# Attention in a two-layer hybrid decoder: the order of scores and transposes on TensorE, and of minimum and copies on VectorE

## The chip, the core and the metric

The kernel runs on one core of one Trainium2 chip. The core has TensorE (matrix products and transposes into PSUM), VectorE, ScalarE, GpSimd and SyncE (which here issues DMAs). Each engine runs its own instructions in program order and waits on semaphores where it needs the work of another. The metric is the device time of one execution in microseconds; lower is better.

## What is computed

A decoder trunk of two layers over 1024 positions of width 1024. Each layer projects its input, sends the columns to three groups (an SSD scan, causal latent attention with 4 heads, sliding-window attention with 4 heads, window 128 and a learned sink for each head), projects their outputs back and then runs a gated MLP. The part that the change touches are the two attentions:

```python
# latent attention, swept over 128-query blocks i, heads h of 4
sc = jnp.einsum('bqhd,bkhd->bhqk', qi, k) * scale          # keys up to block i
sc = jnp.where(kpos[None, :] <= qpos[:, None], sc, -jnp.inf)
pr = jax.nn.softmax(sc, axis=-1)
o  = jnp.einsum('bhqk,bkhd->bqhd', pr, v)

# banded attention: block i sees the key blocks i-1 and i, and a sink
sc = jnp.where(valid, sc, -jnp.inf)
pr = jax.nn.softmax(jnp.concatenate([sc, sink], axis=-1), axis=-1)[..., :-1]
o  = jnp.einsum('bnhgqk,bnkhd->bnqhgd', pr, vb)
```

## The kernel before

In each layer the attention is cut into 32 units (NU), numbered 0 to 31 and written u below. A latent unit ("m") holds one query block and two heads while the block has at most 512 keys, later one head with up to 1024 keys. A banded unit ("s") holds one query block and all four heads. The eight banded units are u = 4, 7, 9, 12, 15, 22, 25 and 28. Everything is float32, and a unit passes through these steps:

- `scores(u)`, TensorE (L1310 for s, L1320 for m): products into PSUM `bank[u % 2]`. It first waits for `un_e` of unit u-2 (L1304), which had that bank. The queries are scaled by a negative number, so a minimum takes the place of the softmax's maximum.
- `least(u)`, VectorE: for m, the mask is taken off the diagonal block in the bank (L2323), then the minimum of each row (L2324). For s, one subtraction carries all four heads from the bank into the SBUF tile `swaProb` (L2316), then the minimum (L2318).
- `exps(u)`, ScalarE: for m, one exponential for each head from the bank into `prob` (L1859), which also waits for the transposes of u-2. For s, four exponentials inside `swaProb` (L1854). The last one signals `un_e`.
- `transposes(u)`, TensorE (L1352 for m, L1347 for s): 128x128 blocks of the probabilities into `bank[2]`. It waits for `un_e` of u and, since there is one bank for all units, for both copies of unit u-1.
- `copy_probs(u)`: the turned blocks go from `bank[2]` to SBUF (L734), one part by ScalarE (`un_ca`), the other by VectorE (`un_cd`).
- `values(u)`, TensorE (L1380 for m, L1371 for s): probabilities times values. An m unit whose head is the first of a pair that is split over two units has none of its own: the second unit does both. Behind the last unit of a query block, `inverse_sums` (L1387) spreads the inverses of the row sums.

ScalarE's order in its loop over u is written out by hand and has a special case: where unit u+1 is latent it runs `exps(u+1)` and then its copy of u; where unit u+1 is banded it runs the copy of u first and then `exps(u+1)`. `finish()` behind them holds small work (the copy of the spread inverses L1872, `att_hi` L1877, and at some units a root or a rounding of SSD outputs). VectorE's loop ends with small work too: the reciprocal of the sums (L2329), the scaling of the outputs (`att_scaled`, L2340) and `att_lo` (L2346), a subtraction of two SBUF tiles.

TensorE's loop before, for each u: transposes(u), scores(u+2), values(u-1), inverse_sums(u-1). VectorE's loop before: copy of u, least(u+2), then the small work. GpSimd meanwhile does other things (adaLN products for the next layer, the SSD outputs' normalisation) that no step here waits for.

The order on ScalarE, which the change leaves as it is:

```python
if u + 1 < NU and UNITS[u + 1][0] == "s":
    copy_probs(act, u, "a", "un_ca")
    exps(u + 1)
    finish()
    continue
if u + 1 < NU:
    exps(u + 1)
if u < NU:
    copy_probs(act, u, "a", "un_ca")
finish()
```

Of the kernel before, what the change touches and what calls it, by code (L numbers as in the profile page):

```python
# [169 lines left out]
NU = len(UNITS)  # L170
# [47 lines left out]
def build(nc, x, c, positions, ada_w, ada_b, norm1_g, norm2_g, w_in, ssd_conv_w, ssd_conv_b,  # L218
# [142 lines left out]
    def half(pair, i):  # L361
        return bank[pair][:, HALF * i:HALF * (i + 1)]
# [17 lines left out]
    def nth(name, v):  # L380

        return passed.get(name, 0) + v
# [293 lines left out]
    def trunk_layer(block, layer):  # L676
# [377 lines left out]
        def _(pe):  # L1054
# [244 lines left out]
            def scores(u):  # L1299
                kind, i, hs = UNITS[u]  # L1300
                if u < 2:
                    pe.wait_ge(s["mp_kv"], nth("mp_kv", 6 + 2 * u))
                else:
                    pe.wait_ge(s["un_e"], nth("un_e", u - 1))  # L1304
                if kind == "s":
                    lo = max(i - 1, 0) * BLK
                    for h in range(SWA_H):
                        r = slice(64 * (h // 2), 64 * (h // 2) + 64)
                        o = bank[u % 2][:, h * 256 + (0 if i else BLK):(h + 1) * 256]
                        last = mm(o, sq[r, h % 2, i * BLK:(i + 1) * BLK], sk[r, lo:(i + 1) * BLK], start=True, stop=True)  # L1310
                else:
                    if u == 0:
                        pe.wait_ge(s["rope_dve"], nth("rope_dve", 3))
                        pe.wait_ge(s["k_rope"], nth("k_rope", 16 * 3))
                        pe.wait_ge(s["mp_q"], nth("mp_q", 12))
                    n = (i + 1) * BLK
                    for q, h in enumerate(hs):
                        for a in range(0, n, HALF):
                            b = min(a + HALF, n)
                            last = mm(bank[u % 2][:, q * HALF + a:q * HALF + b], qh[h][0:96, i * BLK:n], kh[h][0:96, a:b], start=True, stop=True)  # L1320
                last.then_inc(s["un_s"], 1)
# [7 lines left out]
            def transposes(u):  # L1329
                kind, i, hs = UNITS[u]  # L1330
                pe.wait_ge(s["un_e"], nth("un_e", u + 1))
                if u >= 1:
                    pe.wait_ge(s["un_ca"], nth("un_ca", u))
                    pe.wait_ge(s["un_cd"], nth("un_cd", u))
                else:
                    pe.wait_ge(s["mp_kv"], nth("mp_kv", 10))
                if u in SUMS_AT:
                    square_sums(SUMS_AT.index(u))
                if u == TURN_AT:
                    pe.wait_ge(s["sd_rstd"], nth("sd_rstd", 3))  # L1340
                    pe.transpose(half(2, 1)[0:2 * NB, 384:512], rst[:], ident[:])
                if u in NEXT_AT and onward:
                    ada_sum(4 + NEXT_AT.index(u))
                if kind == "s":
                    for h in range(SWA_H):
                        for b in range(0 if i else 1, 2):
                            last = pe.transpose(bank[2][:, (2 * h + b) * P:(2 * h + b + 1) * P], prs[i % 2][:, h, b * P:(b + 1) * P], ident[:])  # L1347
                else:
                    for q in range(len(hs)):
                        for b in range(i + 1):  # L1350
                            c0 = slice(q * HALF + b * P, q * HALF + (b + 1) * P)
                            last = pe.transpose(bank[2][:, c0], pr[u % 2][:, c0], ident[:])  # L1352
                last.then_inc(s["un_t"], 1)
# [29 lines left out]
            def inverse_sums(kind, i):  # L1383

                pe.wait_ge(s["sw_r" if kind == "s" else "ml_r"], nth("sw_r" if kind == "s" else "ml_r", i + 1))
                for h in range(4):
                    last = mm(att_bank(kind)[64 * (h % 2):64 * (h % 2) + 64, 256 + (h // 2) * P:256 + (h // 2 + 1) * P],  # L1387
                              stat[kind][:, i % 3, 2, h:h + 1].to_broadcast([P, 64]), ident[:], start=True, stop=True)
                last.then_inc(s["sw_b" if kind == "s" else "ml_b"], 1)
# [10 lines left out]
            def out_steps(t, ks):  # L1400

                if ks[0] == 0:
                    pe.wait_ge(s["split_lo"], nth("split_lo", splits(N_OUT0 + t)))
                for k in ks:
                    if t == 0:
                        sem, v = ("sd_lo", k + 1) if k < 4 else ("ml_lo" if k < 6 else "sw_lo", NB)
                        pe.wait_ge(s[sem], nth(sem, v))
                    last = dense_step(t, k, tile_of(N_OUT0 + t, wHi), tile_of(N_OUT0 + t, wLo), y_hi_of, y_lo_of, k == 0, k == 5)
                if ks[-1] == 5:
                    last.then_inc(s["pack_used"], 1)  # L1410

            scores(0)
            scores(1)
            for u in range(NU + 1):
                if u < NU:
                    transposes(u)
                if u + 2 < NU:
                    scores(u + 2)
                if u == NU:
                    out_steps(0, (1, 2))  # L1420
                if u >= 1:
                    values(u - 1)
                    kind, i, _ = UNITS[u - 1]
                    if LAST[kind][i] == u - 1:
                        inverse_sums(kind, i)
                if u == NU - 2:
                    out_steps(0, (0,))
# [646 lines left out]
        def _(dve):  # L2074
            step = [0]

            def link(ins):

                step[0] += 1
                ins.then_inc(s["dve_step"], 1)  # L2080
                dve.wait_ge(s["dve_step"], nth("dve_step", step[0]))
# [224 lines left out]
            def least(u):  # L2306
                kind, i, hs = UNITS[u]
                dve.wait_ge(s["un_s"], nth("un_s", u + 1))
                st_ = stat[kind][:, i % 3]
                if kind == "s":  # L2310
                    dve.wait_ge(s["sw_m"], nth("sw_m", 2 + i))
                    if i >= 2:
                        dve.wait_ge(s["un_t"], nth("un_t", LAST["s"][i - 2] + 1))
                    lo = 0 if i else BLK
                    s4 = bank[u % 2][:].rearrange("p (h k) -> p h k", h=4)[:, :, lo:256]
                    link(dve.tensor_tensor(prs[i % 2][:, :, lo:256], s4, band[:].rearrange("p b k -> p (b k)")[:, lo:256].unsqueeze(1).to_broadcast([P, 4, 256 - lo]),  # L2316
                                           ALU.subtract))
                    dve.tensor_reduce(st_[:, 0, :], prs[i % 2][:, :, lo:257], AX.X, ALU.min).then_inc(s["un_n"], 1)  # L2318
                else:
                    n, k = (i + 1) * BLK, len(hs)  # L2320
                    sc = bank[u % 2][:].rearrange("p (q n) -> p q n", q=k)
                    diag = sc[:, :, i * BLK:n]
                    link(dve.tensor_tensor(diag, diag, band[:, 1, :].unsqueeze(1).to_broadcast([P, k, P]), ALU.subtract))  # L2323
                    dve.tensor_reduce(st_[:, 0, hs[0]:hs[0] + k], sc[:, :, 0:n], AX.X, ALU.min).then_inc(s["un_n"], 1)  # L2324
# [24 lines left out]
            def beside_probs(u):  # L2349

                sums = half(2, 1)
                dve.wait_ge(s["un_t"], nth("un_t", u + 1))
                if u == SUMS_AT[1]:
                    dve.tensor_copy(rst[:], sums[:, 384:384 + 2 * NB]).then_inc(s["sd_rstd"], 1)
                if u == TURN_AT:
                    dve.tensor_copy(rstd_row[:], sums[0:2 * NB, 384:512]).then_inc(s["sd_rstd"], 1)
                if u in NEXT_AT and onward:
                    n = NEXT_AT.index(u)
                    dve.tensor_copy(mod[:, n * KT:(n + 1) * KT], sums[:, 384:384 + KT]).then_inc(s["mod_rest"], 1)
# [3 lines left out]
            for u in range(NU + 3):  # L2363
                if u in (SUMS_AT[1], TURN_AT) + NEXT_AT:
                    beside_probs(u)
                if u < NU:
                    copy_probs(dve, u, "d", "un_cd")
                if u == INV_AT:
                    inverse(rst[:], "sd_rstd", 2)
                if u + 2 < NU:  # L2370
                    least(u + 2)
                for w, todo in ((u, inverse_of), (u - 1, att_scaled), (u - 3, att_lo)):
                    if 0 <= w < NU and LAST[UNITS[w][0]][UNITS[w][1]] == w:
                        todo(UNITS[w][0], UNITS[w][1])
# [318 lines left out]
```

## Time and profile before

| | |
|---|---|
| time, 3 runs | 2361.38, 2367.51, 2369.55 us (median 2367.51) |
| the profiled execution's own time | 2360.93 us |
| its span, first to last instruction | 2359.2 us (1.7 us lie around it) |
| mean granted TensorE clock | 0.991 of 2.4 GHz |
| busy share of the span | TensorE 97%, weight loads 79%, VectorE 69%, ScalarE 47%, GpSimd 43% |
| attention of layer 0 | about 350 to 458 us |
| attention of layer 1 | about 1499 to 1604 us |

A row of the timeline is a run of equal instructions: its start, how long from the first start to the last end, engine, line, what it writes and reads, how many. In square brackets stands how long the engine had been idle and who released it. Ends of TensorE's rows are modelled, and a row can overlap the next one by some 0.17 us, since matmuls are pipelined; the distance between two starts is the safer length.

### The profile page before, as it was taken

Reading aid. Unit: us, or ns where it says so; the run is one execution under the profiler, and the core shown is the slowest. Engines: PE = TensorE matmul, PEld = TensorE weight load, DVE = VectorE, ACT = ScalarE, POOL = GpSimd, SP = SyncE. Lnnn points to the kernel's source line nnn. Section 1 sums busy time; section 2 is a strip of 40 time slices with the busy share of each in tenths; the row PEclk is TensorE's granted clock in tenths of the full one; section 3 lists DMA queues with packets and bytes.
Section 4 is the critical chain, followed back from the end, with each engine's and each line's share of the span. In section 5 each row is a group of like instructions: output and inputs, shape, how many; then the busy total and the mean of one; then the engine's idle time right before and its main releaser. Section 6 shows DMA issues by size and latency. Waiting matters only on the chain.

```text
span 2359.2 us, 31193 instructions
## 1 busy us (share of the span) xinstructions
PE 2283.9 (97%) x11493; PEld 1853.1 (79%) x11493; DVE 1633.9 (69%) x2084; ACT 1100.3 (47%) x1808; POOL 1013.5 (43%) x641
## 2 busy tenths in 40 slices
PE   5999999999899999999999999999989999999998
PEld 5788866788788888888878888568878888888887
DVE  6974467638876766777898544773697667677886
ACT  4334646524444444444552454573444444445455
POOL 1211268534887777400002123242479777760000
PEclk7999999999999999999999999999999999999999
DMA  8651213242333333487546331004413333347763
GB/s 292 224 187 54 77 52 126 99 139 85 92 112 90 112 89 118 145 292 254 154 176 206 108 85 54 7 20 152 143 41 125 112 90 112 90 130 254 245 214 112
DMA packets 272533, 310.71 MB, mean 132 GB/s; under 512 B 36872, under 2 KB 191230, under 8 KB 271358
## 3 DMA queue, kind: packets, MB, share of 16 engines
q1 hardware_dynamic: 272094, 307.94, 40.4%
q8 instruction: 92, 1.51, 0.3%
q10 hardware_dynamic: 288, 0.79, 0.2%
q14 instruction: 59, 0.48, 0.1%
HBM read 246.47 MB, written 61.42 MB: 131 GB/s over the span
## 4 chain that ended last, share of the span: by engine, by line
PE 80%; DVE 10%; ACT 3%; issue 2%; POOL 1%; DMA 1%; DVEq 0%; SPq 0%; ACTq 0%; POOLq 0%
PE bank L1489 30%; PE bank L1504 17%; PE bank L1062 15%; PE bank L1122 5%; PE bank L1320 2%; DVE nt L2178 2%; PE bank L1352 1%; PE bank L1280 1%; DVE hLo L2132 1%; PE bank L1380 1%; DVE hLo L2118 1%; DVE xT L2126 1%; DMA raw<-in_ffn_w_up_dram 1%; PE bank L1209 1%; PE bank L1131 1%
## 5 line engine op out<-in xcount | busy, mean ns | idle before, releaser
L982 POOL TENSOR_TENSOR wLo<-raw,wHi 128x1024 fp32r<-128x1024 f32 x66 | 161.9, 2454 | 456.0 <-ACT wHi L984 456.0
L1679 POOL TENSOR_TENSOR prodLo<-comb,prodHi 128x512 fp32r<-128x512 f32 x160 | 234.3, 1471 | 123.6 <-ACT prodHi L1024 123.6
L1489 PE MATMUL bank<-tHi,prodHi 128*128 128x512 f32 x640 | 249.7, 390 | 6.1 <-DVE tLo L2487 4.1
L1489 PE MATMUL bank<-tLo,prodHi 128*128 128x512 f32 x640 | 249.0, 389 | 0.0
L1489 PE MATMUL bank<-tHi,prodLo 128*128 128x512 f32 x640 | 249.0, 389 | 0.0
L1504 PE MATMUL bank<-gateHi,downHi 128*128 128x512 f32 x616 | 240.3, 390 | 0.0
L1504 PE MATMUL bank<-gateHi,downLo 128*128 128x512 f32 x616 | 239.7, 389 | 0.0
L1504 PE MATMUL bank<-gateLo,downHi 128*128 128x512 f32 x616 | 239.7, 389 | 0.0
L1024 ACT ACTIVATE prodHi<-comb 128x512 fp32r<-128x512 f32 x160 | 100.5, 632 | 248.8 <-PE bank L1489 228.7
L2432 DVE SCALAR_TENSOR_TENSOR ub<-bank,ffp,ub 128x1023 f32<-128x1023 f32 x88 | 112.8, 1282 | 141.8 <-ACT ub L1940 140.2
L1489 PE MATMUL bank<-hHi,prodHi 128*128 128x512 f32 x480 | 187.1, 390 | 6.9 <-POOL prodLo L1679 4.3
L1062 PE MATMUL bank<-hHi,wHi 128*128 128x512 f32 x576 | 187.5, 407 | 3.0 <-POOL wLo L982 2.1
L1489 PE MATMUL bank<-hLo,prodHi 128*128 128x512 f32 x480 | 186.8, 389 | 0.0
L1489 PE MATMUL bank<-hHi,prodLo 128*128 128x512 f32 x480 | 186.8, 389 | 0.0
L984 ACT ACTIVATE wHi<-raw 128x1024 fp32r<-128x1024 f32 x66 | 69.5, 1056 | 245.1 <-PE bank L1062 170.2
L1062 PE MATMUL bank<-hLo,wHi 128*128 128x512 f32 x576 | 178.5, 391 | 0.0
L1062 PE MATMUL bank<-hHi,wLo 128*128 128x512 f32 x576 | 177.5, 389 | 0.0
L1679 POOL TENSOR_TENSOR prodLo<-raw,prodHi 128x512 fp32r<-128x512 f32 x120 | 165.3, 1404 | 0.0
L1489 PEld LDWEIGHTS bank<-tHi,prodHi 128*128 128x128 f32 x640 | 120.1, 188 | 33.0 <-DVE tLo L2487 5.0
L1489 PEld LDWEIGHTS bank<-tHi,prodLo 128*128 128x128 f32 x640 | 120.1, 188 | 25.1
L1489 PEld LDWEIGHTS bank<-tLo,prodHi 128*128 128x128 f32 x640 | 120.1, 188 | 24.7
L1504 PEld LDWEIGHTS bank<-gateHi,downHi 128*128 128x128 f32 x616 | 115.7, 188 | 24.4 <-issue 0.8
(392 smaller groups left out, 5402.1 us busy)
## 6 DMA issues: line engine op xcount, KB each, us to landing
raw<-in_ffn_w_up_dram SPq DMA_DIRECT2D x88, 512.0 KB, 5.1
gateRaw<-gateOut SPq DMA_DIRECT2D x154, 256.0 KB, 4.1
adaE<-in_ada_w_dram SPq DMA_DIRECT2D x64, 512.0 KB, 5.7
gateOut<-gateSums SPq DMA_DIRECT2D x22, 1024.0 KB, 5.4
raw<-in_w_in_dram SPq DMA_DIRECT2D x34, 512.0 KB, 4.4
downRaw<-in_ffn_w_down_dram SPq DMA_DIRECT2D x66, 256.0 KB, 3.6
raw<-in_w_out_dram SPq DMA_DIRECT2D x28, 512.0 KB, 4.1
downCols<-in_ffn_w_down_dram SPq DMA_DIRECT2D x24, 512.0 KB, 3.8
```

The costliest lines, as they stand in the source:

```text
L982: eng.tensor_tensor(lo[:], raw[slot][:], fview(hi[:]), ALU.subtract).then_inc(s["split_lo"], 1)
L984: eng.activation((early_hi if n in (N_OUT0, N_PRE + 2) else third_hi if n == 2 else wHi[slot])[:], raw[slot][:], ACT.Copy).then_inc(s["spl ...
L1024: act.activation(sHiW[idx][:], product_source(js, idx), ACT.Copy).then_inc(s["us_hi"], 1)
L1062: last = mm(half(pair, hf), w(k), r(k)[:, HALF * hf:HALF * (hf + 1)], start=first and q == 0, stop=last_k and q == 2)
L1122: last = mm(o, w[n % 2][:, k * P:(k + 1) * P], r(k)[:, cols], start=first and q == 0, stop=last_k and q == 2)
L1131: last = mm(to[:, m:m + 1], acc[:, m * P:(m + 1) * P], caus01[:, P - 1:P], start=True, stop=True)
L1320: last = mm(bank[u % 2][:, q * HALF + a:q * HALF + b], qh[h][0:96, i * BLK:n], kh[h][0:96, a:b], start=True, stop=True)
L1489: last = mm(o, w[idx][:, c0], moving(idx, kp, hi), start=kp == 0 and q_ == 0, stop=kp == 3 and q_ == 2)
L1504: last = mm(down_bank(p, m), w[ring(n)][:, m * P:(m + 1) * P], g[ring(n)][:], start=i == 0 and q == 0, stop=i == NK - 1 and q == 2)
L1679: pool.tensor_tensor(sLoW[idx][:], product_source(js, idx), fview(sHiW[idx][:]), ALU.subtract).then_inc(s["us_lo"], 1)
L2178: ins = dve.scalar_tensor_tensor(out=acc[:], in0=adaE[j][k][:], scalar=cact[:, k:k + 1], in1=acc[:], op0=ALU.mult, op1=ALU.add)
L2432: dve.scalar_tensor_tensor(out=y[:, d:T], in0=bank[2 * q + b][:, 0:T - d], scalar=ffp[:, col:col + 1], in1=y[:, d:T], op0=ALU.mult, op1=AL ...
```

## The change

TensorE issues the scores of unit u+2 ahead of the transposes of unit u, and VectorE runs the minimum of unit u+2 ahead of its copy of unit u. Waits, buffers, the amount of work and the order on ScalarE, GpSimd and SyncE stay.

```diff
@@ TensorE
             scores(0)
             scores(1)
             for u in range(NU + 1):
+                if u + 2 < NU:
+                    scores(u + 2)
                 if u < NU:
                     transposes(u)
-                if u + 2 < NU:
-                    scores(u + 2)
                 if u == NU:
                     out_steps(0, (1, 2))
                 if u >= 1:
@@ VectorE
             for u in range(NU + 3):
                 if u in (SUMS_AT[1], TURN_AT) + NEXT_AT:
                     beside_probs(u)
+                if u + 2 < NU:
+                    least(u + 2)
                 if u < NU:
                     copy_probs(dve, u, "d", "un_cd")
                 if u == INV_AT:
                     inverse(rst[:], "sd_rstd", 2)
-                if u + 2 < NU:
-                    least(u + 2)
                 for w, todo in ((u, inverse_of), (u - 1, att_scaled), (u - 3, att_lo)):
```

## Rows read from the trace of the kernel before

**Rows 1.** The page's part 4: engines' shares of the chain that ended last.

```profile
PE 80%; DVE 10%; ACT 3%; issue 2%; POOL 1%; DMA 1%; DVEq 0%; SPq 0%; ACTq 0%; POOLq 0%
```

**Rows 2.** Windows (length, busy PE, PEld, DVE, ACT, POOL, clock, DMA): both attentions, a pause.

```profile
350.00:458.00 108.00, 102.13 (x901) 74.64 (x901) 81.14 (x144) 74.48 (x206) 85.63 (x40) 1.00 0.30 91
1499.00:1604.00 105.00, 98.81 (x869) 70.80 (x869) 79.68 (x142) 74.49 (x206) 28.86 (x13) 1.00 0.06 20
348.00:353.00 5.00, 3.30 (x19) 2.93 (x20) 1.80 (x5) 2.92 (x12) 4.92 (x3) 1.00 0.35 108
```

**Rows 3.** Waits, 345 to 450 us (waiter, whom for: total us, times, longest).

```profile
PE bank L1352 <- ACT probT L734: 2.5, 3, 1.1
PE bank L1352 <- ACT prob L1859: 2.0, 2, 1.4
PE bank L1347 <- ACT swaProb L1854: 0.8, 1, 0.8
```

**Rows 4.** Timeline, TensorE, around banded unit 12 (transposes 11 to transposes 12).

```profile
388.73 0.74 PE L1352 MATMUL bank<-ident,prob 128*128 128x128 f32 x5 [0.58 <-ACT prob L1859]
389.30 1.25 PE L1320 MATMUL bank<-mlaK,mlaQ 96*128 96x512 f32 x4
390.48 1.09 PE L1380 MATMUL bank<-probT,mlaV 128*64 128x128 f32 x16
391.40 0.61 PE L1387 MATMUL bank<-ident,stat_m 128*64 128x128 f32 x8
392.12 1.09 PE L1347 MATMUL bank<-ident,swaProb 128*128 128x128 f32 x8
```

**Rows 5.** Timeline, ScalarE, same place: copy of 11, first exponential, last accumulator of 12.

```profile
389.50 0.60 ACT L734 ACTIVATE probT<-bank 128x512 f32<-128x512 f32 x1 [0.60 <-PE bank L1352]
389.99 0.50 ACT L1854 ACTIVATE swaProb<-swaProb,stat_s 128x257 f32<-128x257 f32 x1
...
391.87 0.19 ACT L1854 ACTIVATION_READ_ACCUMULATOR swaProb<-swaProb,stat_s 128x1 f32 x1
```

**Rows 6.** Timeline, TensorE, around banded unit 7: transposes 6, values 5, transposes 7.

```profile
370.45 0.85 PE L1352 MATMUL bank<-ident,prob 128*128 128x128 f32 x6
...
372.95 0.88 PE L1380 MATMUL bank<-probT,mlaV 128*64 128x128 f32 x12
373.85 1.09 PE L1347 MATMUL bank<-ident,swaProb 128*128 128x128 f32 x8
```

**Rows 7.** Timeline, TensorE, around banded unit 4: transposes 3, values 2, transposes 4.

```profile
358.39 0.66 PE L1352 MATMUL bank<-ident,prob 128*128 128x128 f32 x4
...
360.27 0.66 PE L1380 MATMUL bank<-probT,mlaV 128*64 128x128 f32 x8
361.06 0.66 PE L1347 MATMUL bank<-ident,swaProb 128*128 128x128 f32 x4
```

**Rows 8.** Timeline, TensorE, around banded unit 15: transposes 14, values 13, transposes 15.

```profile
397.78 0.76 PE L1352 MATMUL bank<-ident,prob 128*128 128x128 f32 x5
...
399.56 1.31 PE L1380 MATMUL bank<-probT,mlaV 128*64 128x128 f32 x20
401.70 1.09 PE L1347 MATMUL bank<-ident,swaProb 128*128 128x128 f32 x8 [0.83 <-ACT swaProb L1854]
```

**Rows 9.** Timeline, TensorE: transposes 21, values 20, and values 26.

```profile
420.43 0.95 PE L1352 MATMUL bank<-ident,prob 128*128 128x128 f32 x7 [1.14 <-ACT probT L734]
...
422.82 1.53 PE L1380 MATMUL bank<-probT,mlaV 128*64 128x128 f32 x24
...
447.30 1.75 PE L1380 MATMUL bank<-probT,mlaV 128*64 128x128 f32 x28
```

**Rows 10.** Timeline, ScalarE: last accumulator of banded unit 22.

```profile
423.79 0.19 ACT L1854 ACTIVATION_READ_ACCUMULATOR swaProb<-swaProb,stat_s 128x1 f32 x1
```

**Rows 11.** Timeline, VectorE, before transposes 20 and 21: att_lo, then the copy of 19.

```profile
414.51 2.38 DVE L2346 TENSOR_TENSOR swaLo<-attOut,swaHi 128x256 fp32r<-128x256 f32 x1
...
416.81 0.41 DVE L734 COPY probT<-bank 128x256 f32<-128x256 f32 x1
```

**Rows 12.** Groups by line, VectorE, 350 to 458 us (busy us, mean ns | idle before).

```profile
L2318 DVE TENSOR_REDUCE stat_s<-swaProb 128x4 f32<-128x1028 f32 (+1 forms) x8 | 9.3, 1157 | 0.3
L2316 DVE TENSOR_TENSOR swaProb<-bank,band 128x1024 f32<-128x1024 f32 (+1 forms) x8 | 9.2, 1152 | 1.9 <-PE bank L1310 1.8
...
L2346 DVE TENSOR_TENSOR swaLo<-attOut,swaHi 128x256 fp32r<-128x256 f32 x7 | 6.2, 890 | 0.0
L2346 DVE TENSOR_TENSOR mlaLo<-attOut,mlaHi 128x256 fp32r<-128x256 f32 x7 | 5.0, 714 | 0.0
```

## The prediction

> **What bounds the kernel now.** First the chain of work that ended last: TensorE holds 80% of it [rows 1]. So a microsecond that TensorE idles inside the attention is a microsecond of the whole, and the question is only what the new order does to TensorE's idle time. Second the windows of the two attentions: TensorE is busy 102.13 of 108 us in layer 0 and 98.81 of 105 in layer 1 [rows 2]. It idles 5.87 and 6.19 us, 12.1 together. That is all a new order can win, 0.5% of the time. Third the waits: what is late is always ScalarE, with its copies (2.5 us), its latent exponentials (2.0) and its banded ones (0.8) [rows 3]. VectorE is late only through it. Last the timeline around a banded unit, where the case is decided.
>
> **What moves.** No instruction is added or taken away. On TensorE scores(u+2) goes ahead of transposes(u), one pass of 1.2 to 1.8 us ahead of one of 0.5 to 1.0. Both wait for the exponentials of u, and the transposes alone also for the copies of u-1. Behind each exponential the chain scores, minimum, exponentials of u+2 starts one transposition earlier, which looks like a gain. But read as a ring the order is now: transposes(u), values(u-1), inverse sums, scores(u+3), transposes(u+1). The exponentials of u+1 were wanted by transposes(u+1), behind all of these; now they are wanted by scores(u+3), one pass of scores sooner.
>
> For a latent unit that costs nothing in steady state: ScalarE runs its exponentials before the copy of u, so they need only the minimum and the transposes of u-1, and are done early. For a banded unit ScalarE's program has the copy of u in front, and this copy needs transposes(u). The chain transposes(u), copy, four exponentials is now wanted at scores(u+3), and between lie only values(u-1) and perhaps the inverse sums.
>
> **The price of one banded unit.** Unit 12 shows the chain bare [rows 4, 5]. Transposes 11 start at 388.73 and last 0.74. The copy starts at 389.50, the first exponential 0.49 later at 389.99, and the last accumulator read ends at 391.87 + 0.19 = 392.06. Transposes 12 start at 392.12, so the chain is 3.39 us, or 2.65 behind the modelled end of the transposes. Unit 22 agrees: 420.43 to 423.79 + 0.19 = 423.98 is 3.55, plus 0.06 is 3.61, minus 0.95 is 2.66 [rows 9, 10]. In rows 4 TensorE filled these 3.39 us with transposes (0.57 between starts), scores 13 (1.18), values (0.92) and inverse sums (0.6), so before it just fits. Take the scores away from between and 1.3 us stay open.
>
> In general the next thing on TensorE can start 0.17 us before a modelled end (0.74 against 0.57, 1.09 against 0.92, both [rows 4]). So the hole is 2.65 + 0.17 = 2.82 us, less the values' busy time less 0.17, less 0.54 where inverse sums stand there (0.61 less 0.07). By unit:
>
> - unit 4: chain 361.06 - 358.39 = 2.67, less 0.66 is 2.01, plus 0.17, less values 0.49: 1.69 [rows 7]
> - unit 7: chain 3.40, less 0.85 is 2.55, plus 0.17, less values 0.71: 2.01 [rows 6]
> - units 9 and 12: 2.82 - 0.92 - 0.54 = 1.36 each [rows 4]
> - unit 15: 2.82 - 1.14 = 1.68 (no inverse sums) [rows 8]
> - unit 22: 2.82 - 1.36 - 0.54 = 0.92 [rows 9]
> - unit 25: 2.82 - 1.58 = 1.24; unit 28: 2.82 - 1.58 - 0.54 = 0.70 [rows 9]
>
> The sum is 10.96 us a layer. The minimum of a banded unit (1.15 + 1.16 us [rows 12]) is asked for before its exponentials by the length of a whole unit, and doesn't lengthen these chains.
>
> **What stays of the old idle time.** The longest wait, 1.4 us for the very first exponentials [rows 3], has nothing that could be put before it and stays. The 0.58 us at unit 11 [rows 4] is a busy ScalarE in front of unit 11's exponentials; it is now met by scores 13: about 0.5. The 0.83 at unit 15 [rows 8] is inside the 1.68 above. The 1.14 at unit 21 [rows 9] begins with an att_lo of 2.38 us [rows 11], and may go or come back.
>
> **What VectorE's half costs.** Its copy of u now stands behind the minimum of u+2. Transposes(u+1) wait for that copy. Between transposes(u) and transposes(u+1) TensorE has values(u-1) and scores(u+3). The worst regular place is u = 20: unit 22 is banded, its minimum takes 2.3 us and unit 19 has no values. From the end of scores 22 VectorE needs 2.3 + 0.1 + 0.4 (copy as in rows 11) = 2.8, and TensorE has transposes 20 and scores 23, some 0.7 + 1.6: 0.5 to 0.6 open. Among the first units, where passes are short, copy 0 behind minimum 2 holds back transposes 1: I lay the first five units out and find 0.7 us of idle where 1.1 was. Bounds for all of VectorE's half: from 0 (all hidden, as most are) to 5.5 us a layer, which is what its att_lo take beyond 0.41 each (11.2 us for 14 [rows 12]), if each such delay now met a waiting TensorE. I take 1.6 (0.6, 0.7 and 0.3 for a late att_lo), nearer zero, because in all of rows 3 no TensorE wait is put down to VectorE.
>
> **Sum.** New idle a layer: 10.96 + 1.4 + 0.5 + 1.6 = 14.5 us. Old: 5.87 and 6.19. Difference 8.6 + 8.3 = 16.9 us. On the profiled execution, 2360.93 us with 1.7 around the span, that is 2377.8. This execution lies at the lower end of the three runs (2361.38 to 2369.55), so against their median the forecast is 2367.5 + 16.9 = 2384.4, given as 2384. Little can absorb it: behind the attention the output projection starts on TensorE without a gap, and its weights are there before.
>
> **Rivals.**
> *The order does what it is shaped for* and the banded hole isn't there, because the copy and exponentials fit beside the values. The old waits but the first go: 12.1 - 2 x 1.4 = 9.3 us, so 2358. For it speaks that the loop scores, minimum, exponentials does get one transposition shorter. Against it stands rows 4 and 5: 3.39 us are measured between transposes 11 and 12, and only 2.1 us of TensorE's work is left in them. It decides if ScalarE's chain were shorter than about 2.1 us.
> *Even:* the stall is there but something later had to wait anyway, so that no more than 7 us arrive at the end: 2367 to 2374. The output projection would have to wait for a weight or for the SSD part, which GpSimd and DMA bring at their own time. Against it: 80% of the chain is TensorE.
> *VectorE becomes the bound:* its att_lo is seen at 2.38 us [rows 11] against some 0.4, and whatever is queued behind it is late. With the minimum now also in front of the copy, both reach transposes(u+1). If all that lock-like time counts, 5.5 us a layer instead of 0.3, the result is 2384 + 10 = 2394. The Trainium skill (page "SBUF — State Buffer", section "Who interferes with whom") has a rule for this that speaks against the change: a VectorE instruction with two SBUF inputs and a GpSimd instruction that reads SBUF exclude each other for a whole instruction. By that rule att_lo (two SBUF inputs) waits and the copies and minima, which have one, don't; the trace agrees, since copies stay at 0.41.
>
> **Chances.** Forecast 0.78, even 0.10, faster 0.06, VectorE as bound 0.06. The forecast's own range: with 1 us less of holes a layer and VectorE's half at zero, 16.9 - 2 - 3.2 = 11.7, from the lowest run 2373; with 2 us more a layer and the highest run, 2369.55 + 20.9 = 2390. For the third rival I reach to 2393. A measurement here can tell about 0.3% (7 us) from no change: faster 0.06, same 0.10, slower 0.84.
>
> **What would show it.** In the changed kernel's waits, scores (L1310 and L1320, two lines on or off) must wait for ScalarE's banded exponentials, eight times a layer and some 11 us in a layer, with 2 us at unit 7 and under 1 at unit 28. The windows of the attentions must be 8 us longer at equal busy time of TensorE. Latent exponentials should release little but at the start. Wrong would be: scores that find the bank free behind banded units; a window that grows while TensorE waits mostly for VectorE's copies; or a granted clock under 1.00 there, which I exclude because it stays at 1.00 where TensorE is busy only 3.30 of 5 us [rows 2].

## The result and the profile after

The changed kernel takes 2382.59 us (median of 4 runs, 2381.83 to 2383.73) where the kernel before took 2367.47 (4 runs, 2361.38 to 2369.55). The recorded ratio is 1.0080, 95% interval 1.0067 to 1.0092, so slower beyond doubt. These two medians alone are only 15.1 us or 0.64% apart, because the four runs of the kernel before scatter by 8 us and three of them lie high: in the runs beside the experiments below (15, 23 and 27 of them) its median is 2364.28, 2364.36 and 2363.70 us, and from those the changed kernel is 18.2 to 18.9 us away. The forecast was 2384, in a range of 2373 to 2393. The execution whose profile is shown took 2382.1 us, 21.2 over the profiled one of before; why that is more than 15.1 is told below.

The page of the changed kernel has the same number of instructions on TensorE, VectorE, ScalarE and GpSimd as before and the same order in the chain that ended last. Its first lines (part 1: busy time, share of the span, instructions) and the chain, which answers to [rows 1]:

```profile
span 2380.3 us, 31195 instructions
PE 2295.1 (96%) x11493; PEld 1863.7 (78%) x11493; DVE 1629.5 (68%) x2084; ACT 1101.0 (46%) x1808; POOL 1013.9 (43%) x641
PE 80%; DVE 10%; ACT 3%; issue 3%; POOL 1%; DMA 1%; DVEq 0%; SPq 0%; ACTq 0%; POOLq 0%
```

The place of the loss is in the windows. I take each attention from the start of its first scores to the start of the output projection behind it. Windows of the changed kernel (length, then busy PE, PEld, DVE, ACT, POOL, granted clock, DMA), layer 0 and layer 1:

```profile
350.40:471.77 121.37, 108.16 (x919) 79.72 (x917) 80.22 (x144) 75.42 (x207) 85.28 (x40) 0.97 0.27 85
1511.46:1625.85 114.39, 101.35 (x886) 73.33 (x885) 77.26 (x142) 75.36 (x207) 29.02 (x13) 1.00 0.06 22
```

The same two stretches of the kernel before:

```profile
350.13:459.16 109.03, 103.16 (x919) 75.53 (x917) 81.27 (x144) 75.11 (x207) 85.50 (x40) 1.00 0.31 95
1498.75:1605.00 106.25, 100.06 (x887) 71.87 (x885) 79.68 (x142) 75.00 (x207) 28.86 (x13) 1.00 0.07 23
```

Layer 0 is 12.34 us longer, layer 1 is 8.14 us longer: 20.5 of the 21.1 us between the two spans. The rest of the program is 0.6 us longer. TensorE's waits in layer 1 of the changed kernel (waiter, whom for: total us, times, longest), to be read against [rows 3]:

```profile
PE bank L1320 <- ACT swaProb L1854: 7.5, 7, 1.4
PE bank L1352 <- DVE probT L734: 2.1, 5, 0.7
PE bank L1310 <- ACT swaProb L1854: 1.7, 1, 1.7
PE bank L1320 <- ACT prob L1859: 1.6, 2, 1.4
```

Before, no scores waited for anything; it was transposes that waited, for ScalarE's copies and exponentials. Now eight scores a layer, lines L1310 and L1320, wait for the exponentials of a banded unit, 9.2 us together. Layer 0 has the same two rows, 7.5 and 1.7. The place of [rows 4] and [rows 5] in the changed kernel, unit 12, TensorE first:

```profile
395.78 0.74 PE L1352 MATMUL bank<-ident,prob 128*128 128x128 f32 x5
396.45 1.09 PE L1380 MATMUL bank<-probT,mlaV 128*64 128x128 f32 x16
397.38 0.61 PE L1387 MATMUL bank<-ident,stat_m 128*64 128x128 f32 x8
399.17 1.35 PE L1320 MATMUL bank<-mlaK,mlaQ 96*128 96x512 f32 x4 [1.19 <-ACT swaProb L1854]
```

and ScalarE and VectorE in the same stretch:

```profile
396.56 0.60 ACT L734 ACTIVATE probT<-bank 128x512 f32<-128x512 f32 x1 [1.48 <-PE bank L1352]
397.05 0.50 ACT L1854 ACTIVATE swaProb<-swaProb,stat_s 128x257 f32<-128x257 f32 x1
...
398.10 0.28 DVE L734 COPY probT<-bank 128x128 f32<-128x128 f32 x1
...
398.93 0.19 ACT L1854 ACTIVATION_READ_ACCUMULATOR swaProb<-swaProb,stat_s 128x1 f32 x1
```

Read it from above: transposes 11 start at 395.78, ScalarE's copy starts as soon as they are done (396.56; ScalarE had idled 1.48 us for them), four exponentials follow without a gap, the read of the last accumulator ends at 399.12, and 0.05 us later scores 14 start. From the transposes' start that is 399.17 - 395.78 = 3.39 us, to the hundredth what [rows 4] showed between transposes 11 and 12. TensorE has values and inverse sums in it, and no longer scores.

The other difference is the clock. In layer 0 TensorE's granted clock falls twice to 0.5, the 1.2 GHz level, which the profiled execution of before doesn't do there. Windows of the changed kernel around the two falls, and most of the stretch between them:

```profile
378.00:382.00 4.00, 4.00 (x31) 3.40 (x30) 3.13 (x4) 1.34 (x5) 2.63 (x2) 0.57 0.46 146
382.00:437.00 55.00, 48.70 (x420) 34.67 (x421) 39.50 (x70) 36.99 (x96) 38.84 (x19) 1.00 0.27 87
439.00:444.00 5.00, 5.00 (x34) 3.83 (x33) 4.05 (x6) 1.93 (x3) 4.37 (x3) 0.66 0.00 0
```

Against full speed the first loses 4 x 0.43 = 1.7 us, the second 5 x 0.34 = 1.7 us. By this estimate 3.4 of layer 0's 12.34 us are clock, and 8.9 are left beside layer 1's 8.14.

### The profile page after: what moved, and what is told of

It reads as the page before. It is cut to its first block, busy times and chain, and to the rows that moved or that the text cites. A ratio compares the mean times of both kernels' runs of the same rounds, so it can differ in the third digit from the quotient of the medians.

```text
span 2380.3 us, 31195 instructions
## 1 busy us (share of the span) xinstructions
PE 2295.1 (96%) x11493; PEld 1863.7 (78%) x11493; DVE 1629.5 (68%) x2084; ACT 1101.0 (46%) x1808; POOL 1013.9 (43%) x641
## 4 chain that ended last, share of the span: by engine, by line
PE 80%; DVE 10%; ACT 3%; issue 3%; POOL 1%; DMA 1%; DVEq 0%; SPq 0%; ACTq 0%; POOLq 0%
PE bank L1489 30%; PE bank L1504 17%; PE bank L1062 15%; PE bank L1122 5%; PE bank L1320 3%; DVE nt L2178 2%; PE bank L1352 1%; ACT swaProb L1854 1%; PE bank L1280 1%; DVE hLo L2132 1%; PE bank L1380 1%; DVE hLo L2118 1%; DVE xT L2126 1%; DMA raw<-in_ffn_w_up_dram 1%; PE bank L1209 1%
```

## The experiments

Theory A is the prediction's: in the new order scores(u+3) want the exponentials of a banded unit u+1, which ScalarE runs only behind its copy of u, and the chain transposes, copy, exponentials (3.39 us) no longer fits under what TensorE has to do. The rivals are named in the expectations. Every ratio is to the kernel before, run on the same chip beside it, with its 95% interval.

### TensorE's half alone

```diff
 (VectorE as before)
+                if u + 2 < NU:
+                    scores(u + 2)
                 if u < NU:
                     transposes(u)
-                if u + 2 < NU:
-                    scores(u + 2)
```

> TensorE's half alone: scores of u+2 ahead of the transposes of u, VectorE in its old order. Theory A (the banded holes: TensorE's scores wait for ScalarE's copy and four banded exponentials, one after the other): the eight holes a layer stay as in the changed kernel, 0.5 to 1.8 us each and 9.2 us together, and only the waits for VectorE's copies (about 2 us a layer) go: 2377 to 2381. Theory B (VectorE's half costs the time, by its late copies): about 2367, as before.

Measured: 2375.97 us, ratio 1.0049 (1.0036 to 1.0061). TensorE's waits in layer 1:

```profile
PE bank L1320 <- ACT swaProb L1854: 7.9, 7, 1.4
PE bank L1310 <- ACT swaProb L1854: 1.7, 1, 1.7
PE bank L1320 <- ACT prob L1859: 1.6, 2, 1.4
PE bank L1310 <- ACT prob L1859: 1.0, 1, 1.0
```

The eight holes are there with VectorE in its old order, so they are TensorE's half: theory B falls as the main cause. The waits for VectorE's copies (2.1 us in the changed kernel) are gone, and one of 1.0 us for a latent unit's exponentials has come. The time is 1 us under the expected band. The rest of the way to 1.0080 belongs to VectorE's half. With falls of the clock taken off (1.7 us in this run's layer 1, 3.4 in the changed kernel's layer 0) its two attentions are 116.6 and 112.6 us long against 117.95 and 114.39: 3.1 us. The 6.6 us between the medians aren't explained by that alone. A second part is probably the clock: the changed kernel's runs have mean clocks of 0.989 to 0.990 and four of these five 0.991 or 0.992. No run here holds the clock fixed, so how the 6.6 us divide stays open.

### VectorE's half alone

```diff
 (TensorE as before)
+                if u + 2 < NU:
+                    least(u + 2)
                 if u < NU:
                     copy_probs(dve, u, "d", "un_cd")
...
-                if u + 2 < NU:
-                    least(u + 2)
```

> VectorE's half alone: minimum of u+2 ahead of the copy of u, TensorE in its old order. The copy now waits for the scores, which stand behind the transposes, and then for a minimum of 1.3 us (latent) or 2.4 (banded); TensorE has only values and inverse sums to cover it. Worked out over the units that is some 0.5 us for most, near 1.9 for each where values are missing (8 a layer) and 1.7 in front of each banded one: 30 us a layer, 2410 to 2440. Theory A expects this, since it holds the two halves for one move that has to be made together. Theory B expects about the changed kernel's 2383.

Measured: 2473.23 us, ratio 1.0458 (1.0444 to 1.0473). The expected direction and cause, but nearly twice the size. TensorE's waits in layer 0, and the window of that attention:

```profile
PE bank L1352 <- DVE probT L734: 24.6, 16, 3.0
PE bank L1347 <- DVE probT L734: 4.3, 5, 1.5
PE bank L1131 <- DVE probT L734: 3.7, 2, 2.3
PE bank L1327 <- DVE probT L734: 3.4, 2, 2.3
PE bank L1341 <- DVE probT L734: 2.0, 1, 2.0
```

```profile
349.76:512.00 162.24, 122.30 (x918) 86.22 (x916) 81.72 (x144) 76.37 (x207) 84.87 (x40) 0.88 0.21 66
```

The waits for VectorE's copies are 38 us in the layer where 30 were worked out. What I had left out is the last column but two: with pauses of up to 3 us the granted clock averages 0.88, and the same products (918 in this window, 919 in that of before) are busy 122.3 us where they were 103.2. Of the 53.2 us by which this attention is longer than before, 34.1 are idle time and 19.1 busy time. The two halves are one move: VectorE's half without TensorE's is far worse than either kernel.

### Old order at the banded unit's own iteration

```diff
+                banded = u < NU and UNITS[u][0] == "s"
-                if u + 2 < NU:
+                if u + 2 < NU and not banded:
                     scores(u + 2)
                 if u < NU:
                     transposes(u)
+                if u + 2 < NU and banded:
+                    scores(u + 2)
 (and the same for VectorE's minimum and copy)
```

> The changed kernel, but at the eight iterations of a layer whose own unit is banded both engines keep the old order (transposes, scores; copy, minimum). Theory A: the scores that had the holes are again behind the transposes, so the holes go and the time is 2360 to 2369. Theory B: 24 of 32 iterations still have VectorE's copy behind the minimum, so most of the loss stays: 2376 to 2382.

Measured: 2380.32 us, ratio 1.0060 (1.0047 to 1.0074). Theory A's expectation failed, by an error of mine, and the time lies where theory B had it. The waits speak against theory B all the same. TensorE's waits in layer 1:

```profile
PE bank L1347 <- ACT swaProb L1857: 9.2, 8, 1.7
PE bank L1352 <- DVE probT L734: 2.3, 4, 0.8
PE bank L1320 <- ACT prob L1862: 1.4, 1, 1.4
```

The holes are all there with their old sizes (9.2 us, eight of them) but stand in front of the banded transposes (L1347). That is what theory A really says: the hole is set by what lies between transposes(u) and the first instruction that needs the exponentials of u+1. Scores(u+2) had already gone ahead of transposes(u), in the iteration before, and it doesn't matter which instruction then meets the wait.

### ScalarE runs banded exponentials first

```diff
-                if u + 1 < NU and UNITS[u + 1][0] == "s":
-                    copy_probs(act, u, "a", "un_ca")
-                    exps(u + 1)
-                    finish()
-                    continue
                 if u + 1 < NU:
                     exps(u + 1)
                 if u < NU:
                     copy_probs(act, u, "a", "un_ca")
```

> The changed kernel with ScalarE's special case taken out: it runs the exponentials of a banded u+1 ahead of its copy of u, as it does for latent units. Theory A: all eight holes a layer go (18.4 us), copies of ScalarE are up to 2 us later at banded units but the scores now lie in front of the transposes that need them; what stays is the first 1.4 us and small waits: 2358 to 2368. Theory C (scores that come early must wait for some exponentials whatever ScalarE's order is, and lost time is the clock's): 2378 or more.

Measured: 2361.76 us (11 runs), ratio 0.9989 (0.9980 to 0.9998), inside the expected band. Its waits in layer 1:

```profile
PE bank L1352 <- DVE probT L734: 2.1, 5, 0.7
PE bank L1320 <- ACT prob L1859: 1.6, 2, 1.4
PE bank L1347 <- DVE probT L734: 0.5, 1, 0.5
```

No wait for a banded exponential is left; the two rows that held 9.2 us are gone, the first two rows are those of the changed kernel, and one wait of 0.5 us for a copy of VectorE has come. Nothing of the change was undone, so its whole loss hangs on ScalarE's order of its copy and its banded exponentials. Theory C falls, its part on the clock too: in this profile the clock falls twice in layer 0, as in the changed kernel's, and the time is still that of before. The same edit on the kernel before is the control:

> The kernel before with nothing but ScalarE's special case taken out. Theory A: before, the chain copy and banded exponentials just fitted under scores, values and inverse sums, so its order is worth little: the 0.8 us at unit 15 and some tenths elsewhere go, but ScalarE's copy is late for the next transposes in places: 2361 to 2368, within 0.15% of before. Theory E (ScalarE's order is worth the same with or without the change): 2350 or less.

Measured: 2369.35 us, ratio 1.0016 (1.0007 to 1.0024): there it costs some 4 us, a little more than expected. The wait for banded exponentials that was to go has grown, from 0.8 us [rows 3] to 1.8 in layer 0. So each order on TensorE has its own best order on ScalarE, and the kernel before had its own.

### The bank given back at the minimum

```diff
-                    pe.wait_ge(s["un_e"], nth("un_e", u - 1))
+                    free = "un_n" if UNITS[u - 2][0] == "s" else "un_e"
+                    pe.wait_ge(s[free], nth(free, u - 1))
```

> The changed kernel with another wait for the scores that follow a banded unit in its bank: they wait for its minimum, which is behind the last read of the bank, and not for its exponentials. ScalarE's order stays. Theory A: the scores go at once and fill the hole; the transposes of the banded unit wait for the exponentials behind scores, values and inverse sums, as before the change. Holes under 0.3 us: 2358 to 2367. Theory C (ScalarE's order itself costs the time, by late copies): 2375 or more.

Measured: 2372.97 us, ratio 1.0034 (1.0021 to 1.0048), only half way: over theory A's 2358 to 2367 and under the 2375 of theory C, which here says that ScalarE's order costs time by late copies. Waits in layer 1 (its lines stand one lower):

```profile
PE bank L1321 <- ACT prob L1860: 3.1, 4, 1.4
PE bank L1353 <- DVE probT L734: 2.1, 5, 0.7
...
PE bank L1311 <- ACT prob L1860: 1.3, 2, 0.7
PE bank L1348 <- ACT swaProb L1855: 0.7, 1, 0.7
```

The scores no longer wait for banded exponentials. But the latent exponentials behind them on ScalarE are late in turn, and the next scores wait for those (1.4 us of the 4.4 are the first unit's, as ever). A part of the hole was handed on, so theory A left something out. Theory C's late copies of ScalarE don't show: no row names them; what is late are exponentials. With ScalarE's order mended as well, the freed bank should add nothing:

> Both mends at once: ScalarE runs banded exponentials ahead of its copy, and the scores behind a banded unit wait only for its minimum. Theory A: with ScalarE's order mended the bank is free in time anyway, so the second mend adds nothing: ratio to before as with the first alone, 0.998 to 0.9998. If waiting for the bank still cost something: under 0.997.

Measured: 2364.08 us, ratio 0.9998 (0.9989 to 1.0007), at the upper edge of the expected band. It isn't better than ScalarE's order alone.

### A longer chain

```diff
                 if u + 1 < NU and UNITS[u + 1][0] == "s":
                     copy_probs(act, u, "a", "un_ca")
+                    if u == 3:
+                        act.wait_ge(s["sd_y"], nth("sd_y", NB))
+                    A(spare[:, UNITS[u + 1][1], :]..., ident[:]..., ACT.Copy)      # 128x256
                     exps(u + 1)
```

> The changed kernel with one more ScalarE copy (128x256, to a tile nobody reads) between its copy of u and the exponentials of a banded u+1. It is worth 0.3 to 0.4 us of ScalarE. Theory A: the chain has no slack, so each of the eight holes a layer grows by just that (1.19 to about 1.55 at unit 12) and the kernel gets 5 to 6.5 us slower than the changed one: a ratio to before of 1.009 to 1.011. If the holes had another cause, ScalarE is busy 46% and would hide it: ratio 1.006 to 1.008 as for the changed kernel.

Measured: 2389.25 us, ratio 1.0108 (1.0094 to 1.0122). Its ScalarE and TensorE at unit 12 (lines a few lower):

```profile
397.10 0.60 ACT L735 ACTIVATE probT<-bank 128x512 f32<-128x512 f32 x1 [1.22 <-PE bank L1353]
...
397.59 0.41 ACT L1900 ACTIVATE spareOut<-ident 128x256 f32<-128x256 f32 x1
397.90 0.50 ACT L1855 ACTIVATE swaProb<-swaProb,stat_s 128x257 f32<-128x257 f32 x1
...
400.02 1.35 PE L1321 MATMUL bank<-mlaK,mlaQ 96*128 96x512 f32 x4 [1.50 <-ACT swaProb L1855]
```

The added copy takes 0.31 us from start to start, and the hole is 1.50 us where it was 1.19. So it is at all eight units: 1.42 became 1.73, 1.74 became 2.04, 1.41 became 1.71, 0.75 became 1.06, 0.97 became 1.28, 0.53 became 0.84. Sixteen times 0.31 is 5.0 us; the medians lie 6.7 apart. The chain has no slack at all, on an engine that is busy 46% of the span.

### Old order one iteration ahead

```diff
+                banded_next = u + 1 < NU and UNITS[u + 1][0] == "s"
-                if u + 2 < NU:
+                if u + 2 < NU and not banded_next:
                     scores(u + 2)
                 if u < NU:
                     transposes(u)
+                if u + 2 < NU and banded_next:
+                    scores(u + 2)
```

With both engines turned back so:

> The changed kernel, but with the old order on both engines in the eight iterations of a layer before a banded unit (u + 1 banded), the other iterations new. Keeping the old order at the banded unit's own iteration moved the eight holes from the scores to the transposes and left their sizes. Theory A, made sharper by that: a hole is 2.8 us less TensorE's work between transposes(u) and whatever first needs the exponentials of u+1. Here scores(u+2) stand between again, 1.2 to 1.8 us, so the holes go or stay under 0.3 us: 2359 to 2367. Theory B (VectorE's half, still new in 24 of 32 iterations): 2374 or more.

Measured: 2383.20 us, ratio 1.0079 (1.0065 to 1.0094). That is far over theory A's 2359 to 2367 and in theory B's band (2374 or more). The holes for banded exponentials are gone but one of 0.33 us, and in layer 1 TensorE now waits like this:

```profile
PE bank L1352 <- DVE probT L734: 9.0, 9, 2.2
PE bank L1320 <- ACT prob L1862: 1.4, 1, 1.4
PE bank L1352 <- ACT probT L734: 0.8, 1, 0.8
```

Where a new iteration is followed by an old one, transposes(u-1) and transposes(u) have no scores between them, and VectorE's copy, which stands behind a minimum, is late: 9.0 us, the size of what was mended. Here theory B is right: this loss is VectorE's half. Another part of the time is clock: in layer 0 of this profile it is at the lower level for 10.2 us in all, an estimated 5.1 us lost. With VectorE's order the old one throughout:

> TensorE's half alone, with TensorE's old order in the eight iterations of a layer before a banded unit; VectorE's order is the old one throughout. The run that did this with both halves lost its gain to VectorE's copies (up to 2.2 us each), because where a new iteration is followed by an old one no scores stand between two transpositions. With VectorE's copy in front of its minimum that can't happen. Theory A: the 18 us of holes of TensorE's half alone (0.49% over before) go, 2358 to 2366, no wait of scores for banded exponentials over 0.3 us. Theory F (a hole just moves to the next unit, whatever is done on TensorE): 2373 or more.

Measured: 2366.52 us, ratio 1.0008 (0.9999 to 1.0017). Of the 0.49% of TensorE's half alone 0.08 are left, so theory F falls; but the median is 0.5 us over the band, and two waits of 0.25 and 0.77 us for banded exponentials stayed in layer 0, where none over 0.3 was expected. Waits of 1.5 to 1.8 us for ScalarE's and VectorE's copies appear at such seams.

### Two candidates

TensorE's half with ScalarE's order mended and VectorE's left alone:

> TensorE's half alone with ScalarE's special case taken out (banded exponentials ahead of the copy), VectorE in its old order. Theory A: no holes from ScalarE, and none of the 2 us a layer that TensorE waits for VectorE's copies when both halves are new: 2 to 4 us under the run with both halves and this ScalarE order, 2356 to 2361. Theory D (with ScalarE's order mended VectorE's half is worth having, since least is then what is late): 2363 or more.

Measured: 2364.58 us, ratio 1.0005 (0.9997 to 1.0014), in theory D's band. The waits agree with it: in layer 1 the scores again wait 2.6 us for banded exponentials, and none did with both halves. And both halves with VectorE's old order only at the first unit and where the unit two on is banded:

```diff
+                late = u == 0 or (u + 2 < NU and UNITS[u + 2][0] == "s")
-                if u + 2 < NU:
+                if u + 2 < NU and not late:
                     least(u + 2)
                 if u < NU:
                     copy_probs(dve, u, "d", "un_cd")
...
+                if u + 2 < NU and late:
+                    least(u + 2)
```

> A candidate: both halves new, ScalarE's special case taken out, and VectorE's old order (copy, then minimum) only at the first unit and at the eight iterations where the unit two on is banded, whose minimum takes 2.4 us. Theory A: of the waits for VectorE's copies that are left with both halves (0.45, 0.3, 0.5, 0.7, 0.4 and 0.3 us, some 2.8 a layer) most go: 2 to 5 us under the run with both halves and this ScalarE order, ratio to before 0.997 to 0.9985. Theory D (these minima are then late for ScalarE): ratio 0.999 or more.

Measured: 2365.73 us, ratio 1.0008 (0.9999 to 1.0017). I was wrong here too: the ratio lies in theory D's band (0.999 or more). Some waits for VectorE's copies are gone, but in layer 0 it waits for exponentials again:

```profile
PE bank L1320 <- ACT prob L1859: 1.8, 2, 1.4
PE bank L1320 <- ACT swaProb L1854: 1.6, 3, 0.8
PE bank L1310 <- ACT prob L1859: 1.4, 2, 1.0
```

With ScalarE's order mended the early minimum is worth having, and the best kernel of all is the changed one with ScalarE's special case removed, 0.11% (0.02 to 0.20) under the kernel before. That gain is barely clear of noise.

## Why the prediction was right

**What bounds the kernel.** Right. The two attentions carry 20.5 of the 21.1 us between the spans, and no later stage took anything back.

**The price of a banded unit.** The mechanism is shown by the holes' place, by the edit of ScalarE's order that removes them, and by the longer chain that enlarges each by its own length. The sizes were 1.69, 2.01, 1.36, 1.36, 1.68, 0.92, 1.24 and 0.70 us; the profile shows 1.42, 1.74, 1.19, 1.19, 1.41, 0.75, 0.97 and 0.53, that is 9.2 a layer in place of 10.96. The chain itself was exact (3.39 us). What was off is the cover, always by the same: 0.27 us where only values stand in it, 0.17 where inverse sums do too. At unit 12 transposes that are followed by values occupy TensorE 0.67 us (395.78 to 396.45), where I had 0.57 from [rows 4], in which scores follow them; and the profile counts a pause from the modelled end, 0.17 us (values) or 0.07 (inverse sums) after the next instruction could have started. The second part is no gain, only another way to count.

**What stays.** The 1.4 us at the first unit stayed (1.38). The 0.5 at unit 11 was 0.23. The wait at unit 15 went into its hole as said.

**VectorE's half.** Taken at 1.6 us a layer; the waits for its copies are 2.1 in layer 1 and 2.3 in layer 0, and with TensorE's half alone the two attentions are 3.1 us shorter, 1.6 a layer. The two places worked out came true: 0.71 us in front of transposes 21 (forecast 0.5 to 0.6), 0.46 at transposes 1 (0.7 in all at the first units). The choice near the lower bound was right, since the upper bound had been 5.5. One reason given for it was too broad: [rows 3] cover layer 0 alone, and in layer 1 of the kernel before TensorE waits 0.9 us for VectorE's copies (two waits, 0.5 and 0.4).

**The sum.** For layer 1, where the clock is full in both profiles, 8.3 us were forecast and 8.14 measured. That is partly luck: the shown waits are 12.9 us where 14.5 were forecast, and busy time grew by 1.3 us (100.06 to 101.35) where I had assumed equal. By line, the latent scores (L1320) are busy 36.6 us in place of 34.8, and all transposes 27.0 in place of 27.8. For layer 0 8.6 were forecast and 8.9 measured with the clock's 3.4 taken off. That 2384 came within 1.5 us of the median measured is luck in part as well. The forecast added its 16.9 us to a median of three runs of before that was 3.2 to 3.8 us higher than the later ones, and holes forecast 1.8 us a layer too large stood against busy time and a clock that it had put at nothing.

**What was wrong.** The last sentence of the forecast excludes a clock under 1.00 in the attention, from one stretch where it had stayed full. It fell twice in layer 0 of this execution. The difference of the profiled executions is 21.2 us; without the clock's 3.4 it is 17.8, 0.9 over the 16.9 of the sum. The medians on record with the result are 15.1 apart, and 18.2 to 18.9 with the later medians of before.

**The rivals.** The gain that the order is shaped for does exist but is small: with the holes mended the whole move is worth 0.11%, where the rival had 0.4%. "Even" fell with the windows. VectorE did not become the bound while TensorE's half was made with it; alone it did, at 1.0458.

## What to carry to other kernels

When an instruction is put ahead of another in a software pipeline, list for every engine that is not touched which of its instructions now lies on the shortened way; here it was a special case for eight units of 32 in ScalarE's order, right for the old order and wrong for the new. The hole can be worked out before a run: the chain's length between two starts, less what the waiting engine still has to do in it, and it doesn't matter which instruction meets the wait. A mend is a change of the other engine's order, not of the place where the wait shows: two attempts to turn the order back locally on both engines only moved the hole, to the transposes or to VectorE's copies, and a third, on TensorE alone, did no more than bring back the time of before. Freeing the bank earlier, where the wait shows, won half.

## What the runs showed of the hardware

The granted clock falls to the 1.2 GHz level within both attentions, in nearly every order of the work that was tried, mostly for some 3.5 us at a time, and such a fall costs an estimated 1.7 us. The longest outside VectorE's half alone lasts 10 us (from 1521 us, ScalarE's order changed in the kernel before). Twelve of the fourteen profiles have stretches in layer 0 or 1 that windows of a microsecond show at 0.50 (366 to 369 and 431 to 434 us with ScalarE's order mended, 1534 to 1537 with TensorE's half alone); the profile of before and that of the second run under "Old order one iteration ahead" have none.

In all profiles but that of VectorE's half alone, each fall begins beside or within 5 us behind one of the groups of 16 products of a single column (L1327 and L1131), of which each profile has four in layer 0 and two in layer 1. With ScalarE's order mended such groups start at 364.18 and 428.52 us and last some 1.9, and the first low windows are those of 366 and 431; in the changed kernel they start at 371.78 and 437.02, and the falls begin at about 378, behind a pause of 1.74 us as well, and at about 439.7. But the 78 groups of these 13 profiles have only 21 falls behind them, and the profile of before has all six groups and no fall. So these groups may have a part in it, and pauses too; no run here takes them apart, and the cause stays open.

It isn't tied to the change. Of the 65 executions of the kernel before beside the experiments, the fastest (2360.58 us) has a mean clock of 0.992 and the slowest (2371.22 us) one of 0.987, and over all of them time and clock go against each other (correlation -0.83), so most of the scatter between its executions goes with the clock.

With pauses of up to 3 us the falls become many: VectorE's half alone, where TensorE idles 40 of 162 us in layer 0, has a mean clock of 0.88 there, with nine falls. The Trainium skill (page "TensorE: Matmul & The Clock Gate", section "HAM oscillation — how this bites in real kernels") tells of a kernel in which the wait for data in each pass of a loop makes the clock fall anew every time. The trace of this run agrees in part: pauses that come again bring falls that come again, but TensorE waits 26 times for VectorE's copies in that layer and the clock falls nine times.
